# Attention of the first block rebuilt: row-packed scores, shares normalised by GpSimd, value tiles stationary under 512 columns

## What is computed

```python
qn = rmsnorm(heads(nq, NSA_HEADS), nsa_qnorm_g[i])          # 8 heads of 64, in 2 groups of 4
q_nope = qn.reshape(B, KVH, G, T, dh)
q_rope = partial_rope(qn, cos, sin).reshape(B, KVH, G, T, dh)
s_cmp = jnp.einsum('bgntd,bgcd->bgntc', q_nope, kc) * scale  # kc: 31 compressed keys
p_cmp = masked_softmax(s_cmp, cmp_mask)
o_cmp = jnp.einsum('bgntc,bgcd->bgntd', p_cmp, vc)
o_slc = selected_attn(q_rope, k_sl, heads(vsl, KVH), sel, scale)
o_win = window_attn(q_rope, k_wn, heads(vwn, KVH), scale)
gates = jax.nn.sigmoid(ngate).reshape(B, T, 3, KVH, G)
o_nsa = gates[0] * o_cmp + gates[1] * o_slc + gates[2] * o_win
y_nsa = o_nsa * jax.nn.silu(nz)
h = h + jnp.concatenate([y_hg, y_nsa], axis=-1) @ w_out[i]
```

## Time and profile before

| | us |
|---|---|
| three executions | 3329.01, 3352.95, 3359.56 |
| median | 3352.95 |
| profiled execution, span on the core | 3356.8 |
| TensorE busy in it | 3082.4 (92%) |
| GpSimd busy | 1906.1 (57%) |
| VectorE busy | 1337.3 (40%) |
| ScalarE busy | 793.8 (24%) |

### The profile page before, as it was taken

How to read it: one execution, slowest core, us unless ns; L and a number is a source line. 1 busy time by engine, 2 the same in 40 slices (tenths; PEclk the granted TensorE clock), 3 DMA queues, 4 the chain that set the end, 5 groups by cost and what they waited for, 6 DMA issues and landing times.

```text
span 3356.8 us, 40413 instructions
## 1 busy us (share of the span) xinstructions
PE 3082.4 (92%) x14668; PEld 2579.2 (77%) x14668; DVE 1337.3 (40%) x1890; ACT 793.8 (24%) x1642; POOL 1906.1 (57%) x885
## 2 busy tenths in 40 slices
PE   5887899988888999889999899999999999899998
PEld 4777787877777878777878678787777878688786
DVE  3766343147663432456432322121456343322021
ACT  2332321233323212312221212010213222222021
POOL 4544200765351007656769568787647769468785
PEclk9999665999986659999999999999989999999999
DMA  5212100222120002322233223332312323223332
GB/s 117 72 35 71 36 1 1 82 75 68 46 66 30 1 3 86 88 66 73 91 94 113 70 72 98 94 95 89 104 51 82 95 93 115 63 81 96 94 94 76
DMA packets 265519, 241.16 MB, mean 72 GB/s; under 512 B 25376, under 2 KB 195424, under 8 KB 265312
## 3 DMA queue, kind: packets, MB, share of 16 engines
q1 hardware_dynamic: 255392, 235.27, 23.9%
q10 hardware_dynamic: 9920, 3.18, 0.5%
HBM read 236.32 MB, written 2.10 MB: 71 GB/s over the span
## 4 chain that ended last, share of the span: by engine, by line
PE 80%; DVE 10%; issue 5%; ACT 4%; SPq 0%; POOL 0%; DVEq 0%; DMA 0%; ACTq 0%; POOLq 0%
PE bank L1629 9%; PE bank L1633 9%; PE bank L1632 9%; PE bank L1587 6%; PE bank L1591 6%; PE bank L1590 6%; PE bank L894 4%; PE bank L674 4%; PE bank L677 3%; PE bank L678 3%; PE bank L917 3%; PE bank L904 2%; PE bank L1559 2%; PE bank L759 1%; PE bank L708 1%
## 5 line engine op out<-in xcount | busy, mean ns | idle before, releaser
L2341 POOL TENSOR_TENSOR whi<-raw,zero 128x1024 fp32r<-128x1024 f32 (+2 forms) x440 | 831.9, 1891 | 1389.1 <-PE bank L674 749.1
L2343 POOL TENSOR_TENSOR wlo<-raw,whi 128x1024 fp32r<-128x1024 f32 (+2 forms) x440 | 1076.0, 2446 | 34.5
L1587 PE MATMUL bank<-xhi,whi 128*128 128x512 f32 x928 | 364.5, 393 | 0.0
L1590 PE MATMUL bank<-xlo,whi 128*128 128x512 f32 x928 | 362.6, 391 | 0.0
L1591 PE MATMUL bank<-xhi,wlo 128*128 128x512 f32 x928 | 362.4, 391 | 0.0
L1629 PE MATMUL bank<-whi,xhi 128*128 128x512 f32 x832 | 329.7, 396 | 11.4 <-DVE xlo L1993 7.6
L1632 PE MATMUL bank<-wlo,xhi 128*128 128x512 f32 x832 | 327.1, 393 | 0.0
L1633 PE MATMUL bank<-whi,xlo 128*128 128x512 f32 x832 | 327.0, 393 | 0.0
L674 PE MATMUL bank<-whi,xhi 128*128 128x512 f32 (+2 forms) x704 | 269.2, 382 | 16.0 <-ACT v L1002 12.8
L677 PE MATMUL bank<-wlo,xhi 128*128 128x512 f32 (+2 forms) x704 | 262.9, 373 | 0.0
L678 PE MATMUL bank<-whi,xlo 128*128 128x512 f32 (+2 forms) x704 | 261.4, 371 | 0.0
(11 more groups left out here) (402 smaller groups left out, 5326.7 us busy)
## 6 DMA issues: line engine op xcount, KB each, us to landing
raw<-in_w_in SPq DMA_DIRECT2D x152, 512.0 KB, 3.6
raw<-in_w SPq DMA_DIRECT2D x132, 512.0 KB, 3.7
raw<-in_w_out SPq DMA_DIRECT2D x16, 512.0 KB, 3.7
raw<-in_w_pg SPq DMA_DIRECT2D x16, 512.0 KB, 3.7
raw<-in_w_o SPq DMA_DIRECT2D x16, 512.0 KB, 3.7
raw<-in_xa_k SPq DMA_DIRECT2D x16, 512.0 KB, 4.0
raw<-in_xa_q SPq DMA_DIRECT2D x16, 512.0 KB, 3.9
raw<-in_xa_v SPq DMA_DIRECT2D x16, 512.0 KB, 3.7
```

Of the source, the lines that this page charges most:

```text
L1587: mm = pe.matmul(o, wh, rhs[0][:, k, :], start=(k == 0), stop=False)
L1590: pe.matmul(o, wh, rhs[1][:, k, :], start=False, stop=False)
L2341: nc.gpsimd.tensor_tensor(whi[:, s, 0:n], raw[:, s, 0:n], zero[:, :].to_broadcast([P, n]), ALU.add).then_inc(hi_split, 1)
L2343: nc.gpsimd.tensor_tensor(wlo[:, s, 0:n], raw[:, s, 0:n], whi[:, s, 0:n].bitcast(F32), ALU.subtract).then_inc(lo_split, 1)
```

## The change

The unit is now a query tile, a group of four heads and a branch: 16 units in a layer. A row is one bank of scores (1, 2, 4 and 4 rows per unit for qt = 0 to 3, 44 rows in a layer). A turn is one key tile of a unit: the four heads' transposes fill one bank of 128 x 512 (40 turns in a layer).

- Scores (line 966) as before, but one mask product for a row (969).
- `weigh`, VectorE (lines 1577, 1578): gate / sum for the four heads of a unit. It stands behind the maximum of the first row of the next unit.
- GpSimd multiplies each row of exponentials by it (line 2428), before the transposes. Its `attention` runs between two weight chunks, those being chunk 2 and chunk 3 of `out0`. It starts by splitting the value tiles (2418, 2421).
- Turn (line 980): ScalarE rounds the bank to the high part (line 1065), VectorE makes the low part (1304).
- Value (lines 991, 992, 993): the value tile of both groups (128 columns) is stationary, 512 columns of four heads pass: three products per turn. Compressed, selected and window branch add up in one bank per query tile and group. The result is already transposed, so the final transposes, the weighting and adding on VectorE (1514 to 1524) go; `y_part` (1590, 1593) multiplies by silu(nz) and splits.
- nz must then be transposed too: `product_turned` (lines 744, 747, 748) has the weights stationary; its chunks are loaded in four DMAs each, and the upper chunks of w_out in two.
- Compressed branch: keys in a block-diagonal tile, `c_score` (936) is 4 products for a query tile where it was 8, `c_val` (954) is 2 products of 512 columns where it was 8 of 64. Its softmax is divided and gated on VectorE ahead of `c_turn` (946).
- All four nz gates stand ahead of the attention. The first chunk of `out0` runs before the last two values.

```diff
+UNITS = [(qt, g, br) for qt in range(TT) for g in range(NKV) for br in range(2)]
+ROWS = [(u, i) for u, (qt, _, _) in enumerate(UNITS) for i in range(NG // HEADS[qt])]
+TURNS = [(u, kt) for u, (qt, _, _) in enumerate(UNITS) for kt in range(qt + 1)]
+P_ROWS, TURN_SLOTS, TURN_LEAD = 8, 3, 2
...
+    for t, (u, kt) in enumerate(TURNS):
+        qt, g, br = UNITS[u]
+        want = min(len(ROWS), rows_of(u)[-1] + 1 + (4 if qt <= 1 else min(4, 2 * kt + 3)))
+        emitted = 0
+        while j < want and (j < P_ROWS or ROWS[j - P_ROWS][0] < u):
+            out += [("score", j)]
+            j += 1
+            emitted += 1
+            if emitted == 1 and kt == 0 and t:
+                out += [("weigh", u)]
...
+        out += [("turn", t)]
+        if t >= TURN_LEAD:
+            out += product(t - TURN_LEAD)
...
-    s += [("c_out",), ("q_rope",), ("nz_gate", 0), ("c_key",), ("p_turn",), ("nz_gate", 1)]
+    s += [("c_out",), ("q_rope",), ("nz_gate", 0), ("nz_gate", 1), ("c_key",), ("p_turn",), ("nz_gate", 2), ("nz_gate", 3)]
+    main, last = attention_steps()
+    out0 = tm("out0", "w_out", 0, 512)
+    s += main + out0[:1] + last[0] + last[1] + out0[1:] + tm("out1", "w_out", 512, 512)
...
+            def step_turn(step):
...
+                if kt == 0:
+                    pe.wait_ge(*pn_ready.at(l, u + 1))
+                pe.wait_ge(*G.free(name, l))
+                for m in range(NG):
+                    mm = pe.transpose(G.ps(name)[:, m * P:(m + 1) * P], p_share(u, m)[:, kt * P:(kt + 1) * P], ident[:, :])
...
+            def step_value(step):
...
+                pe.wait_ge(*G.evacuated(("t", t), l))
+                pe.matmul(G.ps(name)[:, :], vhi[:, kt, br, :], Pt[:, slot, 0, :], start=False, stop=False)
+                pe.matmul(G.ps(name)[:, :], vlo[:, kt, br, :], Pt[:, slot, 0, :], start=False, stop=False)
+                mm = pe.matmul(G.ps(name)[:, :], vhi[:, kt, br, :], Pt[:, slot, 1, :], start=False, stop=CLOSES[t])
...
+            def step_weigh(step):
...
+                dve.wait_ge(*G.evacuated(("s", rows_of(u)[-1]), l))
+                link(nc.vector.reciprocal(coef[:, u % 8, :], sums[:, u % 8, :]))
+                tt_(coef[:, u % 8, :], coef[:, u % 8, :], gts[:, qt, 1 + br, g * NG:(g + 1) * NG], ALU.mult).then_inc(*cf_ready.up())
...
+            def attention(l):
...
+                for u in range(len(UNITS)):
+                    pool.wait_ge(*cf_ready.at(l, u + 1))
+                    heads, n = HEADS[UNITS[u][0]], (UNITS[u][0] + 1) * P
+                    for i, j in enumerate(rows_of(u)):
+                        row = p_row(j)[:, 0:heads * n].rearrange("p (w k) -> p w k", w=heads)
+                        ins = nc.gpsimd.tensor_tensor(row, row, coef[:, u % 8, i * heads:(i + 1) * heads].unsqueeze(2).to_broadcast([P, heads, n]), ALU.mult)
+                    ins.then_inc(*pn_ready.up())
```

More of the change, by code:

```diff
@@ L299, in groups_one, with pieces @@
     if kind == "c_score":
-        return [(("cs", step[1], g), (3 + g,)) for g in range(NKV)]
+        return [(("cs", step[1]), (7, 0, 1))]
     if kind == "c_turn":
-        return [(("cp", step[1], i), (3 + i,)) for i in range(2)]
-    if kind == "c_val":
[L304 to L310, removed]
+        return [(("cp", step[1], g), (7, 0, 1)) for g in range(NKV)]
+    if kind == "score":
+        return [(("s", step[1]), (4, 5, 6))]
+    if kind == "turn":
+        return [(("t", step[1]), (7, 0, 1))]
+    if kind == "c_val":
+        return [(("o_a", *step[1:]), (2, 3))]
     return []
+def pieces(spec):
+    return (0, 1) if (spec[0] == "w_out" and spec[1] >= HG) or (spec[0] == "w_in" and spec[3] == 3864) else (None,)
 def numbered(steps):
@@ L593, in build, with __init__, per @@
         class Ring:
[L596 to L597 removed]
+            def __init__(self, base, chunks, before=None):
+                self.base, self.n = base, len(chunks)
+                self.loads = [len(pieces(c)) * (c[2] if len(pieces(c)) > 1 and c[0] == "w_in" else 1) for c in chunks]
+                self.before = [DEPTH * before.per(s) for s in range(SLOTS)] if before else [0] * SLOTS
+            def per(self, s):
+                return 16 * sum(self.loads[s::SLOTS])
             def loaded(self, l, j):
[L600 removed]
+                s = j % SLOTS
+                return raw_loaded[s], l * self.per(s) + (self.before[s] + 16 * sum(self.loads[s:j + 1:SLOTS]))
             def parts_free(self, l, j):
@@ L728, in step_tm @@
                 kind, i = step[1], step[2]
+                if kind == "nz":
+                    product_turned(step, [(kind, m) for m in range(NG)])
+                    return
                 if i == 0 and kind == "out0":
-                    pe.wait_ge(*G.evacuated(("nT", TT - 1), l))
+                    pe.wait_ge(*G.evacuated(("yT", HG - 1), l))
+                if i == 2 and kind == "out0":
+                    pe.wait_ge(*y_done.at(l, TT))
                 if kind == "pg0":
@@ L922, in step_att @@
-            def step_att(step):
-                i = step[1]
-                if i == 0:
-                    pe.wait_ge(*G.evacuated(("qr", NG - 1), l))
-                for part, *unit in ahead(i):
-                    if part == "s":
-                        scores(*unit)
-                    else:
-                        probs_turn(*unit)
-                values(*UNITS[i])
-            def step_att_turn(step):
-                pe.wait_ge(*y_ready[0].next(l))
-                turn(("nT", step[1]), 4, lambda f: y[:, f * P:(f + 1) * P])
+                pe.wait_ge(*G.evacuated(("cp", qt, g), l))
@@ L1182, in probs, with step_score @@
+            def step_score(step):
+                j = step[1]
+                u, i = ROWS[j]
+                qt = UNITS[u][0]
+                name, n, heads = ("s", j), (qt + 1) * P, HEADS[qt]
+                if j >= P_ROWS:
+                    before = ROWS[j - P_ROWS][0]
+                    act.wait_ge(*G.filled(("t", TURNS.index((before, UNITS[before][0]))), l))
                 act.wait_ge(*nm_ready[0].next(l))
-                for w in range(HEADS[qt]):
+                for w in range(heads):
```

330 lines of the change are left out of this document (183 added, 147 removed).

## The result

The changed kernel takes 3371.36 us in the median of 7 executions (3365.86 to 3372.84), the kernel before 3357.46 beside it (7 executions, 3329.01 to 3363.91). The ratio is 1.0048, 95% interval 1.0024 to 1.0071: slower by half a per cent. That is inside the forecast's "within 1%" and inside the range, but on the other side of 1 than the forecast of 3344.

The account below looks back on a forecast made before the run. TensorE's instructions at half clock were taken to bound the attention. Per layer about 39 us of work leave, about 50 us of waits come, and the clock pays back: 8.6 us less in all, median 3344, range 3295 to 3392.

Parts of the forecast that it names:

- within 1%: Whole kernel: a time of 3319 to 3387, not told from no change by a measurement; chance 0.58.
- What bounds the kernel: Both layers, compressed keys to second norm: TensorE's instructions bound the attention, mostly at half clock; 283.4 us a layer.
- The waits for GpSimd: First turn of each unit: TensorE waits for GpSimd's multiplications, 31 us a layer at half clock, 48 at full.
- Waits of the second kind: Turns in the attention: ScalarE's rounding and VectorE's low part come late, 16 us a layer (0 to 32).
- The start: Before the compressed scores: extra nz gates on ScalarE delay TensorE by 3.5 us a layer (0 to 5.7).
- The compressed values in plain float32: `c_val`: 16 records of 512 columns take 10.3 us a layer, between 6.9 and 13.8, saving 3.6.
- Work that goes: Attention, a layer at half clock: value products, masks, `c_score`, `c_val`, final transposes and a stall save 38.9 us (35 to 43).
- The values: Value products of 40 turns a layer: 69.4 us become 51.6 at half clock, 0.43 per product, saving 17.8.
- The clock: Attention: full clock for 45% of the stage, between 234 us at half and 170 at full clock, giving 205 a layer.
- The rule on transposes: Attention: transposes do not count as busy for the clock, so 3.4 us of them a unit would not raise it.
- the low clock: Rival: attention stays at half clock and GpSimd's waits remain; 49 us more in all, 3402; chance 0.16.
- The high clock: Rival: attention's clock rises nearly throughout, 85%; 60 us less in all, 3293; chance 0.24 with covered waits in it.

Follow-up runs that it names:

- the fastest version: Changed kernel with coefficients made row by row, nz gate 1 behind `c_key` and `p_turn`, first compressed scores behind the second score row: 3214.3 us.
- ten fillers: Changed kernel with ten useless products of 512 columns on TensorE before each unit's wait for GpSimd's multiplications: 3300.0 us, ratio 0.9827 to the kernel before.

## Why the prediction was wrong

- **What bounds the kernel**: right in the main. 9.4 of the 13.6 us lie in the two stretches that were named.
- **The waits for GpSimd**: right in place and cause. Forecast were 31 us a layer at half clock and 48 at full, which is 39 with 45% at full clock; measured 45.9. The multiplication took 1.02 us, near the 1.11 taken from the broadcast row. Three of the four waits at qt = 3 were 3.1 us, between the 2.7 and 4.0 of the forecast, the last 4.7. The eight units of qt = 0 and 1, given 1.6 to 2.5 us each, waited 2.7 in the mean.
- **Waits of the second kind** (turns waiting for ScalarE and VectorE, 16 us a layer): none. The waits after list no such row in layer one. This term was 16 us too high and hid errors the other way. Such waits did appear once the clock was up: 7 us in the fastest version (lines 984 and 995 waiting for DVE Pt).
- **The start**: 5.8 us for the compressed scores, where 1.24 + 3.5 was forecast. The run with the gates moved shows 4 us a layer.
- **The compressed values in plain float32**: 10.3 us a layer forecast at half clock. Two records of 512 columns took 2.0 us at half clock in the timeline (574.42 to 576.42), so 16 of them are 16: above the end that was given (13.8).
- **Work that goes**: right in kind and too large in size. Of the 38.9 us, 33.8 were TensorE's work at half clock. Taken from one start to the next at half clock, about 20 went. The values gave some 9 where 17.8 was forecast: the forecast took 0.43 for each of a turn's three products, but the first takes 0.57 (556.59 to 557.16 in the timeline after), so a turn is 1.42 us there, 1.48 in the mean, and not 1.29. The row for it was there: 585.70 to 586.26 is 0.56 in the earlier trace rows. `c_score` gave 2.4 where 6.9 was forecast, because the old records of 31 columns took about 0.16 in the mean and not the 0.217 of the value records. `c_val` cost 1.6 more where it was to save 3.6. The 36.5 us by which TensorE is busy less include what the clock gave.
- **The clock**: the step that failed. I put 45% of the stage at full clock. The granted 0.65 means 30%, and of 40 turns only 14 had their last value product at full speed (25 at half, 1 between). The difference of 15 points times the 64 us that I gave to the clock is 9.6 us a layer, and the miss inside the stretches is 4.3 + 4.6 = 8.9. That the two agree is luck: the work that goes was some 14 us too large and the waits for GpSimd 7 too small, against the 16 that never came and a few us of small stalls that went without being in the sum. Beside this I counted a share of the whole time, waits included, while 28 of the 70 us at full clock fell into idle time: of the 176 us of work only 42 ran at full clock.
- **The decisive omission**: I treated wait and clock as two terms of a sum, with 45% at full clock whatever the waits. The runs show them coupled: with 44 of the 46 us of waits gone, TensorE's unchanged work also took 36 us less. In the sum, removing the waits was worth 31 to 48 us a layer; it was worth 71. So the forecast of 0.3% less failed in its sign: the clock did not pay the waits back, because the waits took the clock.
- **The rule on transposes** (the Trainium skill, "TensorE: Matmul & The Clock Gate", Part 4): it made the low clock likelier. With ten fillers, units with 16 transposes each ran whole at full clock. So here transposes did not keep the clock down; whether they count as busy is not shown, since other products stood between them.
- **The rivals**: the low clock (3402, slower) named the gap in front of half clock and had the right direction, with about a third of its price (14 us where 49 was forecast), since the clock did come back in part of the units. The high clock did not happen, because of the gaps that were named against it.

## What to carry to other kernels

Price a wait on TensorE with the clock it may take along: here 44 us of waits fewer gave 71 us in a layer's attention, and filling the waits with useless products made the kernel faster. The factor is no constant: 14.8 us less waiting gave 23.5, but 17.9 us more cost only 7.4, because the clock was already down behind most waits. When a slow engine stands in a chain, look first at when it is told: GpSimd had idled 9 to 13 us before each batch at qt = 2 and 3, and giving it each row's coefficient as soon as it existed, not a unit's at the end, was worth 4%. Read the granted clock beside the busy time of the same stretch: full clock that is granted while TensorE waits is no speed. And take the price of the first instruction of a group from its own row: here it was 0.57 us where the ones behind it took 0.43.

## What was not expected of the hardware

- A longer wait cost less than its length: 17.9 us of added waiting in a layer came with 10.6 us less busy time. The time at half clock stayed nearly the same (159 us for 162), and 20 us more of it lay in idle time.
- The clock does not fall as the wait begins: 0.82 was granted over a wait of 3.1 us, and 7.6 us of work behind another wait of that length ran at half clock.
- The same share of idle time (20%) came with a clock of 0.68 in one kernel and 0.81 in another.
- VectorE's multiplication of two SBUF operands by nz (line 1382), 0.68 us otherwise, took 1.36 and 2.27 us beside GpSimd's two splits of the values, which lasted until 371.89 and 374.65. In both cases it ended some 0.55 us behind the end of the split beside it:

```profile
370.00 1.89 POOL L2418 TENSOR_TENSOR vhi<-vv,zero 128x1024 fp32r<-128x1024 f32 x1 [11.17 <-DVE qTr L1304]
371.08 1.36 DVE L1382 TENSOR_TENSOR nzs<-nzs,et 128x512 f32<-128x512 f32 x1 [1.16 <-ACT et L1022]
371.97 2.68 POOL L2421 TENSOR_TENSOR vlo<-vv,vhi 128x1024 fp32r<-128x1024 f32 x1
...
372.93 2.27 DVE L1382 TENSOR_TENSOR nzs<-nzs,et 128x512 f32<-128x512 f32 x1 [0.49 <-ACT et L1022]
```

  The Trainium skill, "SBUF — State Buffer", "Who interferes with whom", says that a VectorE operation with two SBUF inputs contends with a GpSimd operation that reads SBUF; the rows agree, with a slowdown in both (the subtraction took 2.68 where 1024 columns of weights took 2.4 in the median). The 2.27 us stand directly ahead of the low parts of p (line 1304) for which TensorE waited 5.8 us at the start. With the gate moved behind them the wait was 3.1 us, so the order of the gates and the slow multiplication both have a part in it; no run separates them.
